# A hybrid decoder layer: order of the prologue, a convolution tile on VectorE, and the start and end of the down-projection

## What is computed

```
h = RMSNorm(x);  z = h @ W_in + b_in  ->  q, k, v (512 each), cv_a, cv_g (512 each)
A = block-sparse attention (8 heads x 64): blocks of 256 keys, the 3 best past blocks and the own one;
    samples read K and V of 4096 past tokens from a paged cache (32 pages of 128 tokens per sequence)
g = cv_a * sigmoid(cv_g);  c = depthwise causal convolution of 31 taps over g (samples: with 30 rows of state)
C = silu(LayerNorm(c)) @ W_pw + b_pw
x = x + RMSNorm([A, C] @ W_out)
u = RMSNorm(x) @ W_up (1024 -> 5632);  u = depthwise causal convolution of 3 taps (with state)
y = x + RMSNorm((silu(gate) * value) @ W_down)            (2816 -> 1024)
outputs: y, new k and v, new states of both convolutions
```

## Time and profile before

| | |
|---|---|
| median of 3 runs | 1159.12 us |
| profiled execution | 1161.09 us, its span 1159.3 us |
| mean granted TensorE clock | 0.922 of full speed |
| busy: PE, DVE, ACT, POOL | 976.0, 661.5, 446.2, 465.8 us |
| DMA | 205.21 MB, mean 177 GB/s |
| chain that ended last | PE 60%, DVE 14%, POOL 12%, ACT 8%, issue 3%, DMA 2% |

### The profile page before, as it was taken

How to read it: one execution, slowest core, us unless ns; L and a number is a source line. 1 busy time by engine, 2 the same in 40 slices (tenths; PEclk the granted TensorE clock), 3 DMA queues, 4 the chain that set the end, 5 groups by cost and what they waited for, 6 DMA issues and landing times.

```text
span 1159.3 us, 19670 instructions
## 1 busy us (share of the span) xinstructions
PE 976.0 (84%) x7564; PEld 728.1 (63%) x7564; DVE 661.5 (57%) x915; ACT 446.2 (38%) x890; POOL 465.8 (40%) x413
## 2 busy tenths in 40 slices
PE   2498899787878796857979888999999995999995
PEld 1356665353544354535545558999999994777773
DVE  0759584636545467664461336888888886313214
ACT  1315665666576443424231213333333332134323
POOL 1002846748393522350000325456545652133443
PEclk9799899888889798987988898999999998899998
DMA  9679998979797774996934211322232221022232
GB/s 331 218 247 290 313 299 284 323 233 329 257 328 252 265 236 134 320 370 206 326 86 133 86 37 37 99 84 73 75 109 73 73 73 39 35 86 78 73 87 82
DMA packets 155208, 205.21 MB, mean 177 GB/s; under 512 B 10097, under 2 KB 75634, under 8 KB 155072
## 3 DMA queue, kind: packets, MB, share of 16 engines
q1 hardware_dynamic: 154619, 202.33, 52.8%
q10 hardware_dynamic: 495, 1.62, 0.5%
HBM read 198.59 MB, written 5.68 MB: 176 GB/s over the span
## 4 chain that ended last, share of the span: by engine, by line
PE 60%; DVE 14%; POOL 12%; ACT 8%; issue 3%; DMA 2%; POOLq 0%; SPq 0%; DVEq 0%; ACTq 0%
POOL conv L1691 10%; PE tp L839 6%; PE z L839 6%; PE sc L839 5%; PE z L880 5%; PE z L699 5%; PE ob L839 3%; PE sm L839 3%; PE sc L880 3%; PE tp L880 3%; PE z L589 3%; PE sc L511 2%; PE ob L565 2%; PE z L602 2%; DMA wk<-in_w_in 2%
## 5 line engine op out<-in xcount | busy, mean ns | idle before, releaser
L1691 POOL TENSOR_TENSOR conv<-conv,prod 128x576 f32<-128x576 f32 x120 | 170.4, 1420 | 106.2 <-ACT prod L1024 91.1
L1319 DVE STREAM_TRANSPOSE kT<-kN 128x2048 f32<-128x2048 f32 x64 | 145.4, 2296 | 27.8 <-PE sc L511 15.2
L1728 POOL TENSOR_TENSOR wulo<-wu,wuhi 128x2048 fp32r<-128x2048 f32 x22 | 102.5, 4659 | 23.9 <-ACT wuhi L1139 23.9
L1023 ACT ACTIVATE prod<-glu,consts 128x512 f32<-128x512 f32 x124 | 88.9, 717 | 47.8 <-POOL conv L1691 44.7
L1763 POOL TENSOR_TENSOR wdlo<-wd,wdhi 128x1024 fp32r<-128x1024 f32 x22 | 57.4, 2610 | 107.0 <-ACT wdhi L1256 107.0
L1634 DVE TENSOR_TENSOR cvo<-cvo,sg 128x576 f32<-128x576 f32 x22 | 89.3, 4059 | 0.0
L1612 DVE TENSOR_TENSOR fTlo<-fT,fThi 128x1152 fp32r<-128x1152 f32 x22 | 29.8, 1357 | 103.4 <-ACT fThi L1255 99.2
L565 PE MATMUL ob<-vN,pT 128*32 128x128 f32 x2048 | 75.1, 295 | 15.4 <-DMA vN<-in_cache_v 15.4
L602 PE MATMUL z<-hT,wz 128*128 128x512 f32 x192 | 87.7, 613 | 0.0
L565 PEld LDWEIGHTS ob<-vN,pT 128*32 128x32 f32 x2048 | 62.4, 142 | 30.4 <-DMA vN<-in_cache_v 16.8
L511 PE MATMUL sc<-kT,qS 128*32 128x256 f32 x1024 | 70.9, 424 | 5.4 <-DVE kT L1319 5.4
(11 more groups left out here) (297 smaller groups left out, 2569.9 us busy)
## 6 DMA issues: line engine op xcount, KB each, us to landing
kN<-in_cache_k SPq DMA_DIRECT2D x256, 256.0 KB, 4.4
vN<-in_cache_v SPq DMA_DIRECT2D x256, 256.0 KB, 4.0
wu<-in_w_up SPq DMA_DIRECT2D x44, 512.0 KB, 4.6
wd<-in_w_down SPq DMA_DIRECT2D x22, 512.0 KB, 3.6
wz<-in_w_in SPq DMA_DIRECT2D x20, 512.0 KB, 6.4
wo<-in_w_out SPq DMA_DIRECT2D x1, 4096.0 KB, 14.1
wq<-in_w_in SPq DMA_DIRECT2D x1, 2048.0 KB, 15.1
wk<-in_w_in SPq DMA_DIRECT2D x1, 2048.0 KB, 19.8
```

What stands on the lines that cost most here:

```text
L1023: act.activation(dst[:, 0:TP_], glu[:, i, j:j + TP_], ACT.Copy, scale=w_cv[:, i, j:j + 1])
L1319: dve.transpose(kT[:, u % 4, :, :].rearrange("p c (i k) -> p i c k", i=4), kN[:, c % 3, :, :].rearrange("p i (c k) -> p i c k", k=32)).the ...
L1691: ins = pool.tensor_tensor(conv[:, i, :], conv[:, i, :], prod[:, n % 2, :], ALU.add).then_inc(s["prod_used"], 1)
L1728: pool.tensor_tensor(wulo[f % 2][:, :, :], wu[f % 2][:, :, :, :].rearrange("p k u n -> p k (u n)"), wuhi[f % 2][:, :, :].bitcast(F32), ALU ...
```

## The change

- **Prologue.** The prompt's tiles are loaded ahead of `wq` and `wk`, and `wz` ahead of the K pages; all tiles are scaled, transposed and copied before q and k; half of the copies into `qR` are done by ScalarE; the first two gate groups of the convolution stand ahead of the first scores, the other two ahead of the second ones.
- **Convolution.** Channel tile 3 is done by VectorE (`taps` there: multiply and add in one instruction for 512 and one for 64 columns), one tap a step in b = 1, one or two in b = 2 and 3. ScalarE and GpSimd do the other 93 taps: two a step, three and four beside scores.
- **Turned pieces.** VectorE turns two pieces at step 0 and piece u+1 at step u.
- **Samples' tile of the output projection.** Two column tiles of 64 take half of the sum each, side by side; VectorE adds the halves.
- **Down-projection.** The weights get four buffers. Pairs 0 and 1 are split in the last two groups of the up-projection, and TensorE may start on pair 0 four group results earlier. The samples' tile is done in plain float32, unsplit, in two column tiles (two products, not six). The states are transposed after pair 2. The last pair of the left half goes tile by tile; the last two pairs of the right half go together tile by tile, samples first, and the second one's split waits for the end of the pair before.
- **End.** Samples first; VectorE scales and adds both halves; one wait per store.

```diff
+            for t in range(4):
+                sp.dma_start(xA[:, t, :], a["x_prompt"][0, t * P:(t + 1) * P, :]).then_inc(s[f"x_loaded{t}"], 16)
             sp.dma_start(wq[:, :, :], w_in[:, :, 0:DA]).then_inc(s["wq_loaded"], 16)
             sp.dma_start(wk[:, :, :], w_in[:, :, DA:2 * DA]).then_inc(s["wk_loaded"], 16)
-            for t in range(4):
-                sp.dma_start(xA[:, t, :], a["x_prompt"][0, t * P:(t + 1) * P, :]).then_inc(s[f"x_loaded{t}"], 16)
...
+            load_wz(0)
             load_k(0)
             load_k(1)
+            load_k(2)
+            load_wz(1)
+            load_k(3)
             sp.dma_start(wv[:, :, :], w_in[:, :, 2 * DA:3 * DA]).then_inc(s["wv_loaded"], 16)
-            load_k(2)
-            load_wz(0)
-            load_k(3)
-            load_wz(1)
...
+                if n in (2, 3):
+                    sp.wait_ge(s["wu_lo"], FT_N)
+                elif n == 14:
+                    sp.wait_ge(s["y_done"], TT)
+                elif n >= 4:
+                    sp.wait_ge(s["dn_done"], n - 3 if n < 14 else n - 4)
+                sp.dma_start(wd[n % 4][:, :, :], w_dn[:, 2 * kk:2 * kk + 2, nh * TP_:(nh + 1) * TP_]).then_inc(wd_full[n % 4], 16)
...
-            x_tile(0)
+            for i in range(TT):
+                x_tile(i)
...
-            x_tile(1)
...
-            for i in range(2, TT):
-                x_tile(i)
...
+                if t == 4:
+                    for e in range(2):
+                        k = 2 * part + e
+                        for x in range(2):
+                            ins = pe.matmul(Z[nh][64 * x:64 * x + 64, :], mixT[:, 4 * x + k, TP_:TOK],
+                                            wo[:, 4 * x + k, nh * TP_:(nh + 1) * TP_], start=(k == 0), stop=(k == 3))
+                    if part:
+                        ins.then_inc(s["mo_done"], 1)
+                    return
...
+            glu_group(0, 0)
+            glu_group(0, 1)
             pe.wait_ge(s["kown_put"], 1)
             scores(0, 0)
-            glu_group(0, 0)
-            glu_group(0, 1)
+            glu_group(0, 2)
+            glu_group(0, 3)
             scores(0, 1)
             sample_values()
-            glu_group(0, 2)
-            glu_group(0, 3)
...
+            def samples_down(nh, kk):
+
+                for k2 in range(2):
+                    ins = pe.matmul(y_banks[nh][4][64 * k2:64 * k2 + 64, :], fT[kk][:, k2, TP_:TOK],
+                                    wd[(11 * nh + kk) % 4][:, k2, :], start=(kk == 0), stop=(kk == 10))
+                return ins
...
+            def down_pair(nh, kk):
+                down_ready(nh, kk)
+                for t in range(4):
+                    if nh and kk == 0 and t == 3:
+                        pe.wait_ge(s["y0_put"], 2)
+                    for k2 in range(2):
+                        down(nh, kk, k2, t)
...
+                samples_down(nh, kk).then_inc(s["dn_done"], 1)
+
+            def down_last(nh, pairs):
+
+                for kk in pairs:
+                    down_ready(nh, kk)
+                for t in XO:
+                    for kk in pairs:
+                        if t == 4:
+                            ins = samples_down(nh, kk)
+                        else:
+                            down(nh, kk, 0, t)
+                            ins = down(nh, kk, 1, t)
+                    ins.then_inc(s["y_done"], 1)
...
-            pe.wait_ge(s["ux_put"], 4 * FT_N)
-            for nh in range(2):
-                for kk in range(11):
-                    down_pair(nh, kk)
-                    if nh == 0 and kk == 0:
-                        states_to_rows()
+            pe.wait_ge(s["ux_put"], 4 * FT_N - 4)
+            for kk in range(10):
+                down_pair(0, kk)
+                if kk == 2:
+                    states_to_rows()
+            down_last(0, [10])
+            pe.wait_ge(s["ul_put"], 11)
+            for kk in range(9):
+                down_pair(1, kk)
+            down_last(1, [9, 10])
...
                 if b < 4:
-                    taps(3)
-                elif b == 4 and u == 0:
-                    taps(CT * CW)
+                    taps(2)
...
-            act.wait_ge(s["qr_ready"], 1)
+            put_states()
+            act.wait_ge(s["q_put"], 1)
+            qR5 = qR[:, :, :].rearrange("p (h x) t -> p h x t", x=4)
+            for g in (2, 3):
+                for x in range(4):
+                    ins = act.activation(qR5[32 * g:32 * g + 32, :, x, :], qTs[32 * x:32 * x + 32, :, :], ACT.Copy)
+            ins.then_inc(s["qr_ready"], 1)
+            act.wait_ge(s["qr_ready"], 2)
             spread_q(0)
-            put_states()
-            put_scores(0, 0)
             gate_exp(0, 0)
             gate_exp(0, 1)
+            put_scores(0, 0)
             put_scores(0, 1)
...
                     gate_exp(2 * b + 1, 0)
+                    taps(3)
                     gate_exp(2 * b + 1, 1)
                     taps(4)
                 if b in TILES_IN:
+                    taps(4)
+                    put_tile(TILES_IN[b][0])
                     taps(3)
-                    put_tile(TILES_IN[b][0])
-                    taps(2)
...
+            def split_pair(nh, kk):
+                n = 11 * nh + kk
+                act.wait_ge(wd_full[n % 4], 16 * (n // 4 + 1))
+                if n == 0:
+                    act.wait_ge(s["wu_lo"], FT_N - 1)
+                elif n == 1:
+                    act.wait_ge(s["up_done"], 4 * FT_N - 4)
+                elif n == 12:
+                    act.wait_ge(s["y_done"], TT)
+                elif n >= 2:
+                    act.wait_ge(s["dn_done"], n - 1 if n < 12 else n - 2)
+                act.wait_ge(s["ft_ready"], min(2 * kk + 2, FT_N))
+                act.activation(fThi[n % 2][:, :, :], fT[kk][:, :, :], ACT.Copy).then_inc(s["ft_hi"], 1)
+                act.activation(wdhi[n % 2][:, :, :], wd[n % 4][:, :, :], ACT.Copy).then_inc(s["wd_hi"], 1)
...
+                if f == FT_N - 2:
+                    split_pair(0, 0)
+                elif f == FT_N - 1:
+                    split_pair(0, 1)
...
+            for i in range(1, TT):
+                x_scale(i)
+                x_home(i)
...
-            for g in range(4):
+            for g in range(2):
...
+                if t == 4:
+                    for nh in range(2):
+                        cols = slice(nh * TP_, (nh + 1) * TP_)
+                        dve.wait_ge(s["mo_done"], 2 * t + nh + 1)
+                        mo.then(dve.tensor_copy(upperM[0:m, :], Z[nh][64:64 + m, :]))
+                        dve.tensor_tensor(m4[0:m, cols], Z[nh][0:m, :], upperM[0:m, :], ALU.add).then_inc(s["m4_put"], 1)
+                        dve.wait_ge(s["m4_put"], nh + 1)
...
+            def taps(count):
+
+                i = CT - 1
+                gx = glu[:, i, GX:GLUW].rearrange("p (b x) -> p b x", b=NB)
+                dst = conv[:, i, :]
+                ds = dst[:, TP_:TOK].rearrange("p (b t) -> p b t", b=NB)
+                for j in range(tap["n"], min(tap["n"] + count, CW)):
+                    w = w_cv[:, i, j:j + 1]
...
+                    dve.scalar_tensor_tensor(dst[:, 0:TP_], glu[:, i, j:j + TP_], w, dst[:, 0:TP_], ALU.mult, ALU.add)
+                    ins = dve.scalar_tensor_tensor(ds, gx[:, :, j:j + NT], w, ds, ALU.mult, ALU.add)
+                    if j == CW - 1:
+                        ins.then_inc(s["conv_last"], 1)
+                    else:
+                        me.then(ins)
+                tap["n"] = min(tap["n"] + count, CW)
...
+                if b == 1:
+                    taps(1)
+                elif b in (2, 3):
+                    taps(1 + u % 2)
                 if b in HEADS_AT:
...
             gate(0)
+            turn_k(0, 2)
+            turn_k(0, 3)
+            glu_values(0)
             turn_k(0, 4)
+            reduce_scores(0, 0)
             turn_k(0, 5)
-            reduce_scores(0, 0)
             put_sample_values()
-            glu_values(0)
             turn_k(0, 6)
             turn_k(0, 7)
             reduce_scores(0, 1)
...
-                        turn_k(b + 1, u)
+                        for ahead in ((0, 1) if u == 0 else (u + 1,) if u < 7 else ()):
+                            turn_k(b + 1, ahead)
...
+                if f == FT_N - 1:
+                    rest_pair(0)
+                    rest_pair(1)
...
+            def halves_of_samples(nh):
+
+                bank = y_banks[nh][4]
+                dve.wait_ge(s["y_done"], 5 * nh + 1)
+                me.then(dve.tensor_copy(upper[0:TS, :], bank[64:64 + TS, :]))
+                dve.tensor_tensor(y4[0:TS, nh, :], bank[0:TS, :], upper[0:TS, :], ALU.add).then_inc(s["y4_put"], 1)
+                dve.wait_ge(s["y4_put"], nh + 1)
...
+            for i, t in enumerate(XO):
...
+                dve.scalar_tensor_tensor(yo[0:m, t, 0:TP_], y0[0:m, t, :], r2[0:m, t:t + 1], x1[t][0:m, 0:TP_], ALU.mult, ALU.add)
...
-            for n in range(CT * CW):
```

(5 more changed lines are left out.)

232 lines of the change are left out of this document (109 added, 123 removed).

## The result

The changed kernel takes 1145.53 us (median of 4 runs, 1143.27 to 1147.74), beside 1159.69 for the kernel before on the same chip: ratio 0.9865, interval 0.983 to 0.9901. It is faster, as forecast, but by 14 us and not by 32, and outside the range. Its profiled execution took 1147.71, span 1145.9; against the profiled execution before it gained 13.38 us.

The account below looks back on a forecast made before the run. No single bound: DMA in sequence 0, the convolution chain in the middle, TensorE in the FFN. Terms -14.4, +6.0, +3.0, -4.3, -17.5 - 6.2 + 7.0 - 0.7, -4.6 sum to -31.7: 1127 us, range 1108 to 1143.

Parts of the forecast that it names:

- prologue, end of b=0: Sequence 0: scores start earlier and thin DMA stretches fill, so the awaited V page comes earlier; -14.4 us.
- gap and pair 0: Start of down-projection: early splits remove the 14.67 us gap, and pair 0 falls from 9.70 to 6.86; -17.5 us.
- samples' products, 20 pairs: Down-projection: six 64-column matmuls become two side by side, 0.2 us for changing tiles, pair 6.55 us; -6.2 us.
- stop before the last pairs: Down-projection's end: TensorE stops 5.0 us for the second pair's split, then 2 us for a slow clock; +7.0 us.
- tail: After TensorE's end: tiles finish one by one, the last 5.5 us after TensorE instead of 10.1; -4.6 us.
- Pages turned one ahead: Sequences 1 to 5: moved turns delay row sums and last-head softmax, while b=4 loses its last adds; +3.0 us.
- The two waits of +5.8: Sequences 4 and 5: seventh and eighth turns stand ahead of the last head's sums and reciprocal; +5.8 us in each.
- Convolution on VectorE, +6: Sequences 1 to 3: 31 taps on VectorE, about half their instructions meeting a GpSimd add; +6 us, between -11 and +34.
- the fourth rival: Taps blocked and GpSimd's adds stretched to 1.88 us, convolution +64 for +6, slower at 1185 us; chance 4%.
- the first, in which ports hardly matter: Convolution costs nothing and ScalarE's waits go too, -11 for +6: 1110 us; chance 20%.
- The lower bound, -19.4: Sequence 0: the prologue's gain if TensorE alone decides and the DMA gives all of it back; -19.4 us.
- The prediction's second version: Down-projection samples: a tiling-mode drain at both ends costs 0.34 us a pair, making the term -3.6 for -6.2.

Follow-up runs that it names:

- row sums after one turn: Changed kernel, but at step 0 the row sums stand behind one turned piece and the second turn behind them: 1144.35 us, ratio 0.9851.
- both as before: Changed kernel with the early page turns and the convolution tile on VectorE both undone: 1115.73 us, ratio 0.9612.
- small adds: Changed kernel with early turns undone, GpSimd adding only 8 of 576 columns in each of its 90 taps: 1086.01 us, ratio 0.9361.

## Why the prediction was wrong, step by step

| step | predicted | measured |
|---|---|---|
| prologue, end of b=0 | -14.4 | -11.5; with turns as before -16.0; alone -17.7 |
| convolution and turns, b=1 to 5 | +9.0 | +25.7 (to the end of b=7) |
| output projection | -4.3 | -5 |
| gap and pair 0 | -17.5 | -14.7 for the gap, -3.1 for pair 0 (6.56, forecast 6.86) |
| samples' products, 20 pairs | -6.2 | -3.6 |
| stop before the last pairs | +7.0 | 5.1, and 2 for the clock behind it |
| last two pairs and the rest | -0.7 | -1.2 |
| tail | -4.6 | -6.9 |
| from the output projection on | -26.3 | -27.6 |

**The step that failed is "Pages turned one ahead", +3.0.** It asked what stands behind a turn, row sums and the last head's softmax, and priced the turns by their length, 2.3 us. It gave the wait of an early turn for its buffer only to the seventh of b=4 and 5. But the fifth needs a buffer that scores free, too, and waits for it in every sequence from b=1 on, and the seventh in b=4 to 6: 55 us more of standing still in all. Without early turns the kernel is 23.4 us faster, or 26.1 with the convolution as before, where the step's own prices for the turns (2.3 and twice 5.8) make 13.9. The row sums behind two turns, its +2.3, are hardly a part of it (1144.35 against 1145.53). In b=0, where the step had no price, the kernel without early turns is 4.5 faster, but 3.0 of these stand ahead of the first early turn (95.65 against 92.64).

The two waits of +5.8 were seen in kind; the size held in b=4 with the taps on VectorE (5.2; 12.8 without them) and not in b=5. There the wait for the last head came as forecast, 5.98 us at 504.18, but b=5 lost 12.5. First the granted clock of two stretches of b=5 before, then after:

```profile
442.00:452.00 10.00, 3.28 (x15) 2.93 (x16) 8.02 (x17) 4.28 (x11) 1.25 (x1) 0.50 0.06 9
452.00:466.00 14.00, 11.66 (x137) 6.94 (x135) 8.96 (x19) 7.29 (x23) 4.25 (x4) 0.99 0.63 202
```
```profile
442.00:452.00 10.00, 1.75 (x8) 1.57 (x8) 9.65 (x16) 3.09 (x9) 3.22 (x1) 0.51 0.00 0
452.00:466.00 14.00, 13.55 (x99) 8.41 (x98) 5.82 (x12) 6.29 (x18) 0.00 (x0) 0.50 0.62 195
```

In both kernels TensorE stands still for 10.6 us (to 448.27 before, to 450.25 after), and the granted clock is 0.50, the lower of its two levels (1.2 GHz). Before, it is at 0.99 from 452 on; after, it stays at 0.50 for 14 us more, with TensorE busy 13.55 of 14: 99 instructions for 137. Why it came back later wasn't settled, but it is the smaller part: with the convolution as before, and with the row sums after one turn, both with early turns, the stretch at the same place of the sequence has 0.91, and b=5 still lost 10.0 and 10.1.

**Convolution on VectorE, +6.** Its mechanism was right: taps meet GpSimd's adds and wait for their end. In the changed kernel the mean tap is 1.05 + 0.74 = 1.79 us for the 0.98 of one alone. The 10.1 us that were booked to the turned pages for the last adds of b=4 belong here; against the kernel with both as before they came as 7.8. The +6 and -10.1 make -4.1; measured in sum is +0.3 by the profiles and +6.4 by the medians. The wait goes both ways. VectorE, GpSimd and VectorE again in the changed kernel:

```profile
262.30 1.95 DVE L1590 SCALAR_TENSOR_TENSOR conv<-glu,consts,conv 128x512 f32<-128x512 f32 x1
```
```profile
263.85 1.67 POOL L1795 TENSOR_TENSOR conv<-conv,prod 128x576 f32<-128x576 f32 x1
```
```profile
264.17 1.42 DVE L1591 SCALAR_TENSOR_TENSOR conv<-glu,consts,conv 128x64 f32<-128x64 f32 x1
```

The add starts 0.40 us before the first tap instruction ends and lasts 1.67 us for 1.41; the second tap instruction, 0.28 alone, ends with the add. The median add is 1.417 us after and 1.412 before, but 20 of the 90 adds last over 1.5 us (2 of 120 before), and each of these starts while a VectorE instruction with two SBUF operands runs. The Trainium skill, "SBUF — State Buffer", section "SBUF: two separate sides", has the two engines block each other, the one that starts second waiting; the trace agrees. The adds lose some 0.25 us each time, 5 us in all, and the taps 19.6 in the kernel with turns as before. So the fourth rival, in which all adds stretch to 1.88, had the kind and not the size (the longest is 1.74), and the first, in which ports hardly matter, fell to the 19.6 us that the small adds gave back to VectorE.

**Prologue, -14.4.** Right in its mechanism and near in size by itself: -16.0 to -17.7 at the end of sequence 0. In the changed kernel 4.5 of it are lost again: there stand the 6.39 us for row sums at 100.97, late by adds beside the masking and by the second turn, and 2.50 for a page at 129.88; but with the row sums put forward the page came later by as much, so what the early turns do to the loads of b=0 stays open. The lower bound, -19.4, was the better estimate of what it is worth to the whole time.

**Samples' products, -6.2.** The four rows of samples take 1.00 us (1024.92 to 1025.92), not 0.86 + 0.2, but the 24 others take 5.68 to the next samples, not 5.49: 6.68 a pair. The prediction's second version, 0.34 us for a drain at both ends, had 6.69, and the trace agrees with that one in size: 20 x (6.86 - 6.68) = 3.6. The Trainium skill, "TensorEngine Tiling (Array Packing)", section "Key Properties", says that a change of tiling mode drains TensorE; that the drain is what took the time here, no run shows. The 0.2 us that the prediction took from full-width rows between column tiles of 32 were too little.

**Tail, -4.6.** The last addition ends 3.6 us after TensorE, in place of 10.1, and below the 4.2 that were the lower end: -6.5, and -6.9 to the end of the span, better than forecast.

## What to carry to other kernels

Before an instruction is moved ahead in an in-order queue, look up what frees the buffer that it writes: if that event doesn't move, the instruction waits in front of everything that follows it, and its price is what that makes late in each repetition, not its own length. The price isn't the wait itself either: here 55 us more of waiting cost 23 to 26, and in b=2 and 3 of the kernel whose VectorE had no taps it cost nothing. Count a term by the sequence that it repeats in, also where the engine has idle time by its sum; idle time that lies ahead of a wait can't be used behind it. When a change has several parts, run them apart: here prologue and FFN carried 45 us, and turns and convolution gave some 30 of them back.

## What the runs showed of the hardware

- VectorE instructions with two SBUF operands and GpSimd's adds waited for each other: a tap of 64 columns took 0.28 us alone and up to 1.43 beside an add of 1.41, and the 20 adds that started during such a VectorE instruction took 1.66 to 1.74.
- With a stop of TensorE of the same length ahead of it (10.6 us), the granted clock stayed at 0.50 for 10 us in one kernel and for 24 us in another.
- Full adds on GpSimd held sequences 1 to 3 some 9 to 10 us each above what they take with small ones (68.3, 68.1 and 66.7 us against 58.4, 59.4 and 57.3), and with those the DMA was busy 97% of the time, at 326 GB/s.
